# Weight rows of three stages laced in pairs and read with step two, and three stages that stream their moving operand backwards

## What is computed

```python
f = (jax.nn.silu(g) * (h @ w_up)) @ w_down            # first block, stage "down"
merged @ w_out_2                                      # second block, stage "out2"
q = jnp.einsum('td,dhk->thk', xb, w_q)                # PEER, stage "wq"
u = u_emb[expert]                                     # PEER, stage "U"
a = jax.nn.gelu(jnp.einsum('thkd,td->thk', u, xb).astype(jnp.float32), approximate=False)
coef = (g * a).astype(xb.dtype)
return jnp.einsum('thk,thkd->td', coef, v_emb[expert])   # PEER, stage "V"
```

## Time and profile before

| | |
|---|---|
| median of three executions | 3399.2 us |
| profiled execution, its own time | 3402.69 us |
| its span, first to last instruction | 3400.8 us |
| PE busy | 3366.7 us (99%), 24828 matmuls |
| PEld busy | 3185.5 us (94%), 24828 loads |
| DVE busy | 2176.9 us (64%) |
| ACT busy | 1673.4 us (49%) |
| mean granted TensorE clock | 0.994 of 2.4 GHz |

### The profile page before, as it was taken

The page is one execution under the profiler, slowest core; times in us unless marked ns, Lnnn a source line. Parts: engine busy times, 40 slices in busy tenths (PEclk is TensorE's granted clock), DMA queues, the critical chain, the costliest instruction groups (busy, mean ns, idle before and its releaser), DMA issues.

```text
span 3400.8 us, 60220 instructions
## 1 busy us (share of the span) xinstructions
PE 3366.7 (99%) x24828; PEld 3185.5 (94%) x24828; DVE 2176.9 (64%) x3664; ACT 1673.4 (49%) x2630; POOL 100.3 (3%) x131
## 2 busy tenths in 40 slices
PE   8999999999999999999999999999999999999998
PEld 8999999999999999899999999999999998888887
DVE  8865377666654476565566788877755555555655
ACT  5454454444444444544454444566644444444544
POOL 0000100000000100000000000122100000000000
PEclk9989999999999999999999999999999999999999
DMA  6433445555556655444565555544455555556554
GB/s 206 139 116 118 159 158 187 184 181 184 184 181 189 186 164 175 131 137 161 180 195 194 193 184 187 171 146 147 156 187 187 187 189 188 190 191 223 190 190 161
DMA packets 164000, 593.12 MB, mean 174 GB/s; under 512 B 18448, under 2 KB 19088, under 8 KB 163344
## 3 DMA queue, kind: packets, MB, share of 16 engines
q1 hardware_dynamic: 163728, 589.27, 53.0%
HBM read 585.00 MB, written 4.19 MB: 173 GB/s over the span
## 4 chain that ended last, share of the span: by engine, by line
PE 98%; DVE 1%; DMA 1%; ACT 0%; issue 0%; SPq 0%; ACTq 0%
PE ps L774 31%; PE ps L775 31%; PE ps L776 31%; PE ps L1258 2%; PE ps L841 1%; PE ps L1062 0%; DMA raw<-in_peer_v 0%; PE ps L1034 0%; PE ps L883 0%; PE ps L811 0%; PE ps L1089 0%; PE ps L843 0%; PE ps L1088 0%; DMA raw<-in_w_in 0%; PE ps L1099 0%; PE ps L1084 0%
## 5 line engine op out<-in xcount | busy, mean ns | idle before, releaser
L2089 ACT CAST wh<-raw 128x1024 fp32r<-128x1024 f32 (+2 forms) x1116 | 1158.2, 1038 | 1328.9 <-PE ps L776 1325.3
L1330 DVE TENSOR_TENSOR wl<-raw,wh 128x1024 fp32r<-128x1024 f32 (+2 forms) x1116 | 1349.4, 1210 | 535.7 <-ACT wh L2089 533.5
L774 PE MATMUL ps<-xh,wh 128*128 128x256 f32 (+2 forms) x5184 | 1487.9, 287 | 20.0 <-DVE xl L1339 10.2
L775 PE MATMUL ps<-xl,wh 128*128 128x256 f32 (+2 forms) x5184 | 1472.0, 284 | 0.0
L776 PE MATMUL ps<-xh,wl 128*128 128x256 f32 (+2 forms) x5184 | 1469.5, 283 | 0.0
L774 PEld LDWEIGHTS ps<-xh,wh 128*128 128x128 f32 x5184 | 987.3, 190 | 26.2 <-issue 10.7
L775 PEld LDWEIGHTS ps<-xl,wh 128*128 128x128 f32 x5184 | 986.2, 190 | 2.3
L776 PEld LDWEIGHTS ps<-xh,wl 128*128 128x128 f32 x5184 | 985.8, 190 | 0.0
L774 PE MATMUL ps<-wh,ch 128*128 128x512 f32 x1024 | 403.7, 394 | 0.8 <-DVE cl L2026 0.8
L775 PE MATMUL ps<-wl,ch 128*128 128x512 f32 x1024 | 403.1, 394 | 0.0
L776 PE MATMUL ps<-wh,cl 128*128 128x512 f32 x1024 | 402.9, 393 | 0.0
(11 more groups left out here) (361 smaller groups left out, 3172.9 us busy)
## 6 DMA issues: line engine op xcount, KB each, us to landing
raw<-in_peer_u SPq DMA_DIRECT2D x256, 512.0 KB, 4.1
raw<-in_peer_v SPq DMA_DIRECT2D x256, 512.0 KB, 4.5
raw<-in_w_in SPq DMA_DIRECT2D x186, 512.0 KB, 3.7
raw<-in_w_up SPq DMA_DIRECT2D x82, 512.0 KB, 4.3
raw<-in_w_gate SPq DMA_DIRECT2D x80, 512.0 KB, 4.3
raw<-in_w_down SPq DMA_DIRECT2D x80, 512.0 KB, 3.8
raw<-in_w_out SPq DMA_DIRECT2D x64, 512.0 KB, 3.8
raw<-in_w_branch_a SPq DMA_DIRECT2D x16, 512.0 KB, 3.5
```

The costliest lines, as they stand in the source:

```text
L774: t.matmul(o, lh, rh, start=start, stop=False)
L775: t.matmul(o, lh, rl, start=False, stop=False)
L1330: v.tensor_tensor(wl[:, i % SN, 0:cols(i)], raw[:, i % RN, 0:cols(i)], wh[:, i % SN, 0:cols(i)].bitcast(F32), ALU.subtract).then_inc(lo, 1)
L2089: s.copy(wh[:, i % SN, 0:cols(i)], raw[:, i % RN, 0:cols(i)]).then_inc(hi, 1)
```

## The change

The change touches addresses only. No instruction is added, removed or moved on any engine: TensorE, VectorE, ScalarE, GpSimd and SP have the same instructions in the same order, with the same waits.

- **Lacing.** On the host the rows of `w_down`, `w_out_2` and `peer_u_2` are laced in pairs: of two weight rows of 128 floats that stood one behind the other, the elements now alternate. `row_at` reads a row of the pair with step two. A stationary operand of down, out2 and U so spreads over 1024 bytes of each partition, not 512. The DMA, the cast and the subtraction treat the chunk as before.
- **Coefficients.** For groups with an odd number n the two token halves are laced in the same way in `ch` and `cl`: ACT and DVE write them with step two, and TensorE reads them with step two. For even n they stay contiguous. The moving place now advances with `n // 2 % 16`, so that even and odd groups each go through all 16 places.
- **Backwards.** In out2, in wq and in half 1 of V the moving operand is read from its last column to its first, and the result is written in the same order, so that each column lands where it did.

```diff
+LACE = {"down": 1, "out2": 1, "U": 1}
...
-    def coef_at(x, n, c0=0, w=S):
-
-        o = 320 * (n % 2) + 4 * (n % 16) + c0
-        return x[:, o:o + w]
+    def row_at(w, i, r):
+
+        name = PLAN[i][0]
+        if name not in LACE:
+            return w[:, i % SN, 128 * r:128 * r + 128]
+        return w[:, i % SN, 256 * (r // 2):256 * (r // 2) + 256].rearrange("p (g h) -> p h g", h=2)[:, r % 2]
+
+    def coef_at(x, n):
+
+        o = 320 * (n % 2) + 4 * (n // 2 % 16)
+        if n % 2:
+            return x[:, o:o + S].rearrange("p (g q) -> p q g", q=2)
+        return x[:, o:o + S].rearrange("p (q g) -> p q g", q=2)
+
+    def coef_in(n):
+        return G[:, n % 128, :].rearrange("p (q g) -> p q g", q=2)
...
-                c = slice(128 * (k - k0), 128 * (k - k0) + 128)
-                last = three(o, wh[:, i % SN, c], wl[:, i % SN, c], *rhs(k), start and k == k0, stop and k == k0 + n - 1)
+                last = three(o, row_at(wh, i, k - k0), row_at(wl, i, k - k0), *rhs(k), start and k == k0,
+                             stop and k == k0 + n - 1)
...
-                chunk(O2 + 2 * m + c, ps[m % 4][:, 0:S], 8 * c, 8, lambda k: (mg[0][:, k, :], mg[1][:, k, :]), c == 0, c == 1,
+                chunk(O2 + 2 * m + c, ps[m % 4][:, 0:S][:, ::-1], 8 * c, 8, lambda k: (mg[0][:, k, ::-1], mg[1][:, k, ::-1]), c == 0, c == 1,
...
-                chunk(WQ + 2 * m + c, ps[m % 4][:, 0:S], 8 * c, 8, x3, c == 0, c == 1,
+                chunk(WQ + 2 * m + c, ps[m % 4][:, 0:S][:, ::-1], 8 * c, 8, lambda k: (xh[:, k, 0:S][:, ::-1], xl[:, k, 0:S][:, ::-1]), c == 0, c == 1,
...
+                back = slice(None, None, -1 if half else 1)
+                last = three(acc(half, qt, b)[:, back], coef_at(ch, n)[:, qt], coef_at(cl, n)[:, qt], wh[:, i % SN, dd][:, back],
+                             wl[:, i % SN, dd][:, back],
...
-            v.tensor_tensor(coef_at(cl, n), G[:, n % 128, :], coef_at(ch, n).bitcast(F32), ALU.subtract).then_inc(c_l, 1)
+            v.tensor_tensor(coef_at(cl, n), coef_in(n), coef_at(ch, n).bitcast(F32), ALU.subtract).then_inc(c_l, 1)
...
-            s.copy(coef_at(ch, n), G[:, j, :]).then_inc(c_h, 1)
+            s.copy(coef_at(ch, n), coef_in(n)).then_inc(c_h, 1)
...
+def laced(w, n):
+
+    m, p, k = w.shape
+    return np.ascontiguousarray(w.reshape(m, p, k // 256, 2, 128 // n, n).transpose(0, 1, 2, 4, 3, 5)).reshape(m, p, k)
...
+    for name, key in (("w_down", "down"), ("w_out_2", "out2"), ("peer_u_2", "U")):
+        A[name] = laced(A[name], LACE[key])
```

More of the change, by code:

```diff
@@ L1298, in v_tile @@
                 dd = slice(512 * b, 512 * b + 512)
-                last = three(acc(half, qt, b)[:], coef_at(ch, n, 128 * qt, 128), coef_at(cl, n, 128 * qt, 128), wh[:, i % SN, dd], wl[:, i % SN, dd],
+                back = slice(None, None, -1 if half else 1)
+                last = three(acc(half, qt, b)[:, back], coef_at(ch, n)[:, qt], coef_at(cl, n)[:, qt], wh[:, i % SN, dd][:, back],
+                             wl[:, i % SN, dd][:, back],
                              j == 0, j == 127)
```

## The result

| | before | after |
|---|---|---|
| median of three executions | 3399.2 us | 3422.8 us (3419.8 to 3424.99) |
| ratio to before, with its 95% interval | | 1.0066 (1.0043 to 1.0089) |
| profiled execution | 3402.69 us | 3419.8 us |
| its span | 3400.8 us | 3418.0 us |

A forecast was written before the change was run, and what follows sets the result against it. The prediction took TensorE, busy 99% of the span, as the bound. From the profiled 3402.7 us it took 39.8 us for down and U, all else 0, and 3.5 to the median: 3359.4, so 3360 us, range 3325 to 3455.

The forecast's parts named there:

- Only the distance between starts can move the time: TensorE: only a changed distance between two matmul starts, or a new wait of PE, could move the time.
- The two reads disturb each other, as their addresses stand to each other: TensorE: moving read and weight load disturb each other by 0 to some 5 ns per matmul, depending on addresses.
- My figure for V half 0: V half 0, window 2850 to 3100 us: 231.4 ns per matmul.
- Step two: both streams advance at one pace, so their distance stays as it is; at best it goes to out2's 113.3 ns. I take the best end: Down and U, forwards: 113.3 ns per matmul, gaining 30.7 us in U and 9.1 in down, together 39.8 us.
- The equal-pace argument: Down and U: a step-two load covers 1024 bytes like the moving operand, so both advance together; gain 39.8 us.
- rival C: Down, U, out2, odd V groups: twice the memory per load, twice the disturbance; 51 us slower, 3450 us; chance 0.28.
- Out2, "I take 0": Out2, step two with backwards: nothing to win, a loss of 3.8 us at U's level; taken as 0.
- V, "I take 0": V, step two in odd groups: bounds -7.4 and +7.4 us, taken as 0; half 1 backwards also 0.
- rival D: Backwards results or strided loads run at a fraction of the pace; doubled distance in half 1, out2, wq 488 us; chance 0.05.
- Step two in the coefficients, "the price is 0": V's odd groups: ACT and DVE write ch and cl strided under cover, price 0; without cover 51 us.
- The rule of two hits on a 16-byte line: SBUF loads: step two in float32 has exactly two hits, so a load does not get slower.

The follow-up runs named there:

- fixed_places: The kernel before with compact moving rows in down, in2, wq and U at one remainder, and V's coefficients at two fixed places; 3355.0 us, ratio 0.9865.
- fixed_places_2: fixed_places with the activation rows of in2, wq and U 512 bytes further on; 3353.0 us, ratio 0.9859.
- fixed_places_3: fixed_places_2 with the compact activation rows of in2, wq and U at remainder zero modulo 512 bytes; 3393.9 us, ratio 0.9983.
- lace_only: The changed kernel without its backwards half: lacing and step two kept, all operands and results forwards; 3422.2 us, ratio 1.0058.
- result_back: fixed_places_2 with only the results of down, out2, wq, U and V half 1 written last column to first; 3351.5 us, one execution.
- back_only: The kernel before with only the backwards half: out2, wq and V half 1 read and write last column to first; 3408.4 us, ratio 1.0021.
- moving_back: fixed_places_2 with only the moving operand of down, out2, wq, U and V half 1 read backwards; 3388.6 us, one execution.
- lace_and_back: fixed_places_2 with lacing and backwards reads in down, out2 and U, and V half 1 backwards; 3386.7 us, one execution.

## Why the prediction was wrong

**"Only the distance between starts can move the time": right.** PE's shares and chain did not change. PE's wait for `cl` was 0.2 us in all.

**"The two reads disturb each other, as their addresses stand to each other": right, and now shown.** `fixed_places` gains 46 us by places alone. Places of both operands count: within V of the kernel before only the coefficients, the stationary operand, change their place, and the groups stand at 226.7 to 234.4 ns; from `fixed_places_2` to `fixed_places_3` only the moving operand of in2, wq and U does, and U goes from 115.7 to 119.9. That it is the distance between the two, and not each one's own address, fits all runs, but no run moved both together. The Trainium skill (TensorE: Matmul & The Clock Gate, Part 2, step 1) says that the two operands come through independent ports and that a load takes no read bandwidth from the running matmul; 113.3 to 120.0 ns for the same instructions at other addresses do not agree with it. My figure for V half 0 was taken from a window whose last part lies in half 1, which begins at 3033.3 us. The stage means of 232.0 and 231.4 differ little from its 231.4, so nothing hung on it.

**"Step two: both streams advance at one pace, so their distance stays as it is; at best it goes to out2's 113.3 ns. I take the best end": this step failed.** I took a load with step two for the same process with another path through memory, which could find the good relation. The runs show a form that the good relation does not reach: 120.0 ns in down, out2 and U and 233.3 ns in V at the places that give a contiguous load 113.3 and 226.7, and on average nearly the same with walking places (120.2 in down, 119.6 in U, 232.5 in the odd groups of V). In its place the term is this: U 6144 x (119.6 - 118.2) = +8.9 us and down 2112 x (120.2 - 117.6) = +5.3 us, where I had -30.7 and -9.1. The rows could not have told me the level. They could have told me that I had no row with a strided load, and that the best end of a bound for an unseen form is a hope. The equal-pace argument had only out2 behind it, and out2's load does not keep pace with its stream.

**The size of rival C** (51 us, measured 21.5) came from doubling each stage's own disturbance. But step two is not added on top of what a stage already pays: the 256-column stages all end near 120 ns in `lace_only`. So the price is the less, the worse a stage stood before: 1.4 ns in U, 2.5 in down, 6.7 in out2 in `lace_only`. On good places the same lacing costs 54.8 us.

**Out2, "I take 0": wrong**, +3.5 us, close to the 3.8 that I gave as its bad end. It was the one stage at the low level, so it had everything to lose. There the backwards read even softened the loss, from 120.0 to 117.8.

**V, "I take 0": nearly right**, +3.7 us in all: 2.7 in odd groups and 1.0 in even ones. In the kernel before its places already had it at 231 to 232, so there was little left to lose.

**Backwards, and rival D.** The form is not dear. The Trainium skill (PSUM — Partial Sum Buffer, Specifications) says that non-contiguous patterns slow matmuls significantly; a result written backwards, if it counts as one, cost nothing in `result_back`, 113.3 and 226.7 ns. What costs is the read of the moving operand, and little. In `back_only` it was worth 3.4 us in out2 and 2.7 us in V half 1 (3.8 by the distances alone, without a wait of about 1 us that the profile of before has and this one has not); in the change out2's took the place of lacing's 5.1.

**Step two in the coefficients, "the price is 0": right.** ACT and DVE in V half 1 after, groups of lines of 3150 to 3350 us, against the earlier trace rows:

```profile
L2042 DVE TENSOR_TENSOR cl<-G,ch 128x256 fp32r<-128x256 f32 x72 | 30.6, 425 | 41.2 <-ACT ch L2477 41.2
...
L2477 ACT CAST ch<-G 128x256 fp32r<-128x256 f32 x71 | 29.7, 418 | 92.5 <-PE ps L790 92.5
```

425 stays 425, and 406 became 418 ns, with 92.5 us of idle time in front of ACT. The mean hides that only odd groups pay: over half 1, ACT takes 405 ns in even groups and 432 in odd ones, and before it took 405 and 406.

**The rule of two hits on a 16-byte line** (the Trainium skill, SBUF — State Buffer, Specifications) fits both forms roughly: step two of float32, with two hits, costs 6.7 ns per matmul at the held places, and step four, with one, doubles its time. I had used it to say that a load does not get slower. It is shown 7 ns longer in U of `lace_only` than before (196 against 189 ns). That the matmuls pay for this length is not shown: between 1950 and 2150 us U stands at 117.8 ns in `moving_back` with loads of 188 ns and in `lace_and_back` with loads of 193, and in `fixed_places_3` at 120.0 ns with contiguous loads of 192.

**Left open.** Why step two never comes near 113.3 ns is not settled; whether it is the load's own reading or a clash with the moving read was only argued. That the backwards read lowers it to 117.8, and that in V it depends on the place (229.9 to 233.7), speaks for a clash. Step two was held at one place per stage only; a sweep might find a better one. In which direction the load runs was not tried. A stationary operand of contiguous pieces of 16 bytes was not tried either.

## What to carry to other kernels

When TensorE is the bound and each matmul has its own load, divide a full window by its count of starts, stage by stage: stages of one shape with different distances point to operand places, and a pitch and a start offset can win (1.4% here, `fixed_places_2`), where no form of access tried here won anything. Find the stage that already runs at the lowest distance and give the others its pitch and offset; change no form of access there. A form that no row shows may not reach the best distance at all: try it in one stage before a sum is built on the good end of its bounds.

## What the hardware showed unasked

- With the places held, the distances come in levels. At 2.4 GHz, 113.33, 117.78 and 120.0 ns are 272, 282.7 and 288 cycles for 256 columns, and 226.67 and 233.33 ns are 544 and 560 cycles for 512.
- Equal addresses can run at two levels. U of `fixed_places_2` stands at 113.3 ns from 1880 us on. At 2007.5 us three matmuls of 128 columns (`ident,G`) come between two chunks of U, and from there it stands at 117.8. At 2143.5 us three more come, and it falls back to 113.3 (some 114 ns while groups of `oh` and `par` matmuls stand between its chunks). From the first group of V at 2419.9 us on it is 117.8 again. So V's groups are not the only thing that switches it, as I had supposed before `fixed_places_3`. Windows at either level, before any matmul of V, columns as in the earlier trace rows:

```profile
1880.00:2000.00 120.00, 120.00 (x1061) 120.00 (x1060) 105.83 (x277) 56.13 (x70) 0.00 (x0) 1.00 0.58 189
2010.00:2130.00 120.00, 120.00 (x1021) 120.00 (x1021) 103.98 (x268) 54.48 (x67) 0.00 (x0) 1.00 0.59 188
```

The mean of U is therefore 115.7 and not 113.3. V half 0 shows the same in `lace_and_back`: the groups between U's chunks stand at 231.2 ns and the later ones at 226.7, where `fixed_places_2` has 226.7 in both, though nothing in V half 0 was changed. What sets the level once a stretch begins stays open. Rows of the timeline of PE in `fixed_places_2`, three matmuls in 0.34 us, and later six in 0.71:

```profile
1960.23 0.28 PE L776 MATMUL ps<-xh,wh 128*128 128x256 f32 x1
...
1960.57 0.28 PE L776 MATMUL ps<-xh,wh 128*128 128x256 f32 x1
...
2601.67 0.28 PE L776 MATMUL ps<-xh,wh 128*128 128x256 f32 x1
...
2602.02 0.28 PE L776 MATMUL ps<-xh,wh 128*128 128x256 f32 x1
...
2602.38 0.28 PE L776 MATMUL ps<-xh,wh 128*128 128x256 f32 x1
```

- The width of the moving operand changes which places are good. In the kernel before, groups of V at remainder zero (modulo 512 bytes) ran at 226.8 ns per matmul, the best of all, while remainder zero at 256 columns gave 120.0 in `fixed_places_3`, the worse of the two that were held.
- Backwards, the places matter less: in V half 1 of the changed kernel 29 of the 32 places stand at 233.1 to 233.9 ns and three at 236.3 to 236.7, where forwards, in the kernel before, they range from 226.7 to 234.4. No place is good any more, and a few are worse than any forwards.
